# One conditioned hybrid decoder layer on 8 cores: places of its own for two row tiles, first evictions first, and a new planned order

## The reference

```python
mod = silu(c) @ w_ada + b_ada                       # six vectors: sh1, sc1, gt1, sh2, sc2, gt2
h = rmsnorm(x, norm_mix_g) * (1 + sc1) + sh1
x_rnn, y_rnn, u_pool, g_a, g_b = split(h @ w_in)    # five projections 1024 -> 1024
xr = causal_conv(x_rnn, conv_w, conv_b)             # width 4
hr = rg_lru(xr, ...)                                # gates by 4 diagonal blocks, h_t = a_t h_(t-1) + b_t
branch_a = (gelu(y_rnn) * hr) @ w_branch_a
branch_b = multiscale_pool(u_pool, ...) @ w_branch_b
x = x + gt1 * ((sigmoid(g_a) * branch_a + sigmoid(g_b) * branch_b) @ w_out)
h = rmsnorm(x, norm_mlp_g) * (1 + sc2) + sh2
x = x + gt2 * (relu(h @ w_up) ** 2 @ w_down)        # 1024 -> 4096 -> 1024
out = rmsnorm(x, final_g)
```

## Time and profile before

| what | value |
|---|---|
| runs before | 1187.74, 1188.84, 1207.44 us; median 1188.84 |
| profiled execution | 1189.46 us; span of its slowest core 1187.9 us |
| spans of the cores | 1180.7 to 1187.9 us |
| granted TensorE clock, mean of a core | 0.972 to 0.980 |
| busy | PE 1063.4 us (90%), DVE 716.0 (60%), ACT 685.5 (58%), POOL 244.6 (21%) |

### The profile page before, as it was taken

One profiled execution on the slowest core, in us unless ns is written; L12 is line 12 of the kernel. 1 busy time (PEld: TensorE's weight loads), 2 busy tenths in 40 slices (PEclk: granted clock), 3 DMA queues, 4 the chain that ended last, 5 costly groups with the idle time before them and its releaser, 6 DMA issues.

```text
span 1187.9 us, 16767 instructions; the slowest of 8 cores (1180.7 to 1187.9 us)
## 1 busy us (share of the span) xinstructions
PE 1063.4 (90%) x5262; PEld 492.6 (41%) x5262; DVE 716.0 (60%) x1060; ACT 685.5 (58%) x1054; POOL 244.6 (21%) x307
## 2 busy tenths in 40 slices
PE   0256687999999899899799999999999999999996
PEld 0123343444444344344344444444444444444442
DVE  4457877953666968977787686136403556070446
ACT  2267888575969788547888037930364211626354
POOL 2403343210413243222221013100000000022145
PEclk9888798999999999999999999999999999999998
DMA  9999775853265484416226512704030321001013
GB/s 272 229 195 203 181 193 159 232 162 119 39 161 125 71 214 88 117 27 148 45 73 199 209 72 48 131 1 72 1 71 14 58 41 31 1 18 54 18 71 124
DMA packets 46230, 127.34 MB, mean 107 GB/s; under 512 B 3888, under 2 KB 11456, under 8 KB 43840
## 3 DMA queue, kind: packets, MB, share of 16 engines
q1 hardware_dynamic: 21920, 90.82, 22.7%
q0 software_dynamic: 24224, 35.46, 20.7%
HBM read 144.93 MB, written 29.37 MB: 147 GB/s over the span
## 4 chain that ended last, share of the span: by engine, by line
PE 77%; DMA 7%; issue 5%; DVE 4%; ACT 3%; SPq 2%; POOL 1%; POOLq 0%; DVEq 0%; ACTq 0%
PE ps L579 75%; DMA w_bb<-w_b 4%; DMA ada<-w_adaT 2%; SPq L547 2%; DMA xt<-xin 1%; DVE xr L561 1%; PE ps L659 1%; ACT a L553 1%; ACT poolB L553 1%; DVE a L561 1%; POOL stat L568 1%; PE ps L912 0%; ACT L553 0%; DVE xrb L561 0%; PE ps L1094 0%
## 5 line engine op out<-in xcount | busy, mean ns | idle before, releaser
L561 DVE TENSOR_TENSOR ps<-ps,gtb 128x512 f32<-128x512 f32 x160 | 111.8, 699 | 253.1 <-PE ps L579 253.0
L579 PE MATMUL ps<-h2T,wup 128*128 128x512 bf16 x1024 | 223.5, 379 | 0.2 <-ACT h2T L553 0.2
L579 PE MATMUL ps<-wdn,ff 128*128 128x512 bf16 x1024 | 222.6, 379 | 0.0
L553 ACT ACTIVATE ps<-ps 128x512 f32<-128x512 f32 x128 | 74.0, 584 | 183.4 <-PE ps L579 183.0
L561 DVE SCALAR_TENSOR_TENSOR xr<-ps,vecs,xr 128x510 f32<-128x510 f32 (+2 forms) x192 | 135.7, 742 | 57.6 <-ACT xr L553 54.3
L579 PEld LDWEIGHTS ps<-wdn,ff 128*128 128x128 bf16 x1024 | 100.1, 98 | 120.9 <-issue 0.3
L579 PEld LDWEIGHTS ps<-h2T,wup 128*128 128x128 bf16 x1024 | 99.9, 98 | 119.8 <-issue 0.3
L561 DVE TENSOR_TENSOR x<-ps,x 128x512 f32<-128x512 f32 x160 | 110.3, 691 | 15.8 <-DVE ps L561 1.2
L568 POOL TENSOR_TENSOR thi<-thi,a 128x1024 f32<-128x1024 f32 x32 | 79.2, 2481 | 172.0 <-ACT a L553 101.1
L561 DVE TENSOR_TENSOR_SCAN a<-thr,hst,thi 128x512 f32<-128x512 f32 x64 | 85.9, 1377 | 17.3 <-POOL thi L568 17.2
L568 POOL TENSOR_SCALAR stat<-stat 128x1 f32<-128x1 f32 x65 | 18.0, 277 | 348.4 <-ACT xn L553 196.8
(11 more groups left out here) (125 smaller groups left out, 1435.5 us busy)
## 6 DMA issues: line engine op xcount, KB each, us to landing
wTb<-w_adaT SPq DMA_DIRECT2D x32, 512.0 KB, 5.2
xt<-xin SPq DMA_DIRECT2D x29, 512.0 KB, 6.9
ada<-w_adaT SPq DMA_DIRECT2D x16, 512.0 KB, 18.2
x<-xin SPq DMA_DIRECT2D x16, 512.0 KB, 10.5
yout<-x SPq DMA_DIRECT2D x16, 512.0 KB, 2.6
wdn<-w_dn POOLq DMA_DIRECT2D x6, 1024.0 KB, 13.9
wup<-w_up POOLq DMA_DIRECT2D x6, 1024.0 KB, 14.3
q_h<-hTm SPq DMA_DIRECT2D x4, 1024.0 KB, 5.6
```

The source lines that it names most:

```text
L553: N.add("act", lambda e: e.activation(out=out() if callable(out) else out, in_=in_() if callable(in_) else in_, func=func, **kw), reads=re ...
L561: return m(**args)
L579: ins = e.matmul(ps[tok.bank][:, lo:hi], lhsT=l, rhs=r, start=(first and i == 0), stop=(last and i == n - 1))
```

## The change

The rank of the first prefix tile's transposes and evictions goes from -4 to -10, so that they fall under the rule of `first`. Row tiles 2 and 3 of prefix tile 1 are loaded to two new places, `xq0` and `xq1`, which lie where `wTb1` and `wTb2` are later; tiles 0 and 1, and all rows after, keep `xt0` and `xt1`. The planner's duration of a 128x128x512 matmul is 0.2165 in place of 0.222 us and that of a transpose 0.1 in place of 0.11. `HOW` has a tilt of 14 in place of 5, three refinements in place of none, and five seeds in place of two, so the sequence of every engine is another one. The computation is the same.

```diff
-HOW = (5.0, 0, (5000001, 5000181))
+HOW = (14.0, 3, (14800055, 14800067, 14800071, 14800072, 14800142))
...
-            N.add("pe", fn, reads=reads, writes=[tok], us=0.222 * len(pairs) * (hi - lo) / 512, rank=rank, soft=soft)
+            N.add("pe", fn, reads=reads, writes=[tok], us=0.2165 * len(pairs) * (hi - lo) / 512, rank=rank, soft=soft)
...
+        xq = [at(f"xq{i}", [P, D], F32, MG + (8 + 4 * i) * K1) for i in range(2)]
+        for i in range(2):
+            reg(f"xq{i}", MG + (8 + 4 * i) * K1, 4 * K1)
+
         def norm_sub(row, s, rank):
             if row < 512:
                 t, k = xt0[s], f"xs{s}"
+            elif 512 <= row < 1024 and s > 1:
+                t, k = xq[s - 2], f"xq{s - 2}"
             else:
                 i = n_x[0] % 2
                 n_x[0] += 1
...
-                N.add("pe", tr, reads=[f"xn{s}" for s in range(nsub)] + ["ident"], writes=[tok], us=0.11 * nsub, rank=rank, soft=[keys[c]])
+                N.add("pe", tr, reads=[f"xn{s}" for s in range(nsub)] + ["ident"], writes=[tok], us=0.1 * nsub, rank=rank, soft=[keys[c]])
...
-            make_hT(T * TT, 4, lambda c: hTp[T][:, c, :], hp(T), T - 0.9 if T > 1 else -0.6 if T else -4)
+            make_hT(T * TT, 4, lambda c: hTp[T][:, c, :], hp(T), T - 0.9 if T > 1 else -0.6 if T else -10.0)
```

## The result

The changed kernel takes 1193.81 us (median of five runs, 1192.79 to 1195.48) against 1188.84 us before: a ratio of 1.0048, interval 1.0032 to 1.0064. A second series of the same file, on another chip, gave 1.0037 (1.0022 to 1.0052). So it is slower by 4.4 to 5.7 us. That is far under the 2% named in the prediction and inside its range, but on the other side of no change than the 1179.4 us forecast. Some executions of every kernel here are slow ones, with half of the chip or more at a lower granted clock; the ratios, and the times given for the experiments, are of the others.

The account below looks back on a forecast made before the run. Bound: full DMA, then ACT and DVE, with TensorE waiting, in the head; casts on DVE from 400 to 600 us. 1189.5 - 0 - 5.5 - 4 = 1180.0, or 1179.4 us for the median; range 1163 to 1197.

Parts of the forecast that it names:

- part 3: New planner order and durations, 400 to 600 us: casts on DVE set closer to the need, 4 us gained.
- Part 1: First tile's evictions go first: projections start 3.2 us earlier, at 51.1, waited away by 85 us; gain taken as 0.
- Part 2: Own places for two row tiles: x rows land earlier, TensorE's stop at 113.7 to 121.8 us goes; 5.5 us gained.
- rival (a): The forecast itself: the x-buffer stop goes and later stalls shrink, 1179.4 us (1173 to 1186); chance 0.50.
- the ring: Two xt buffers shared by nine x-row loads; with two tiles out, last main row lands near 93 instead of 119.2 us.
- rival (e): New order leaves the x loads behind the wTb wait, same time as (b); chance 0.20 together with (b).
- (b): Head: the transfer is hidden anyway, ACT and DVE take over as bound, 1188.8 us; chance 0.20, shared with rival (e).
- (c): Head: two early x rows displace weights by 5.4 us, restart at half speed adds 1.8: 1196.0 us; chance 0.15.
- (d): Search finds much more: full 9.9 us in the head and 15.2 us from 400 to 600: 1163.7 us; chance 0.13.
- Last x row before 100: Sign of being right: the last of the nine x loads lands before 100 us.
- No stop over 4 us from 100 to 130: Sign of being right, in the head: TensorE has no stop over 4 us between 100 and 130 us.
- The MLP's stretch unchanged in length: Sign of being right: the MLP, where TensorE had no idle time from 900 to 1000 us, keeps its length.

Follow-up runs that it names:

- a_wy: Changed kernel, order kept, w_y loaded in two column halves, each with its own semaphore: 1184.8 us against 1185.7 before the change, ratio 0.9997.
- a_cast: Changed kernel, order kept, four of POOL's converting copies beside the w_y load moved later: 1189.4 us against 1186.0 before the change, ratio 1.0029.
- a_wy_wb0: Changed kernel, order kept, w_y in two halves and first half of w_b behind the w_gb loads: 1181.8 us against 1185.7 before the change, ratio 0.9966.
- b_evict: Kernel before, order kept, ACT's two evictions of hTp moved ahead of the two Squares: 1188.0 us against 1186.2, ratio 1.0013.
- b_xq_sp: Kernel before, order kept, two row tiles in own places, last two x-row loads ahead of wTb loads on SP: 1187.2 us against 1186.2, ratio 1.0012.
- a_wb0: Changed kernel, order kept, first half of w_b moved behind the two w_gb loads on POOL: 1187.3 us against 1185.7 before the change, ratio 1.0016.
- a_same: Changed kernel run once more, unaltered, beside later experiments: 1191.2 us against 1186.7 before the change, ratio 1.0037.

## Why the prediction was wrong, point by point

**The step that failed is part 3**, the term of 4 us (bounds +8.2 lost, 15.2 gained). I read it from the stalls of the stretch from 400 to 600 us alone. That reading was right as far as it went: 15.2 us of idle time became 9.1, "less than 12" as the text asked, and xrb's waits 12.0 became 2.4. But I took everything outside this stretch as unchanged, and never asked what slack of the old order the new one might spend. The old order had over 38 us between the landing of w_y and its first use (45.6 in the plan); the new one has 0.3 us by the planner's price of 11.4 us for the load. The chip gave 11.3 to 19.0 us, so the load is late on five of eight cores by 2.6 to 8.0 us, and the slowest core sets the time. *a_wy* shows it as the cause of the 0.4%: with nothing else changed the loss is gone and the cores are as near each other as before. One doubt is left: in *a_cast* no core waits for w_y either, and the ratio stays at 1.0029. There w_ga is late on four cores and the head spreads the cores by 6.6 us, but no run takes these apart. The gain that the term stands for is there as well: with both late loads mended, *a_wy_wb0* is 4.0 us faster than the kernel before. That this equals my 4 us is luck in part, since no run shows which of its stages gives it. My lower bound, "one more stall of the longest kind, 8.2 us", had the right size by luck; it named a stall of DVE, and I gave it no chance of its own as a rival. No forecast case said that a load just in time is late on some cores.

**Part 1** was right in the trace and in the sum. Start forecast at 51.1, measured 51.71; worth 0, and *b_evict* alone gives 1.0013, with its start at 49.48. In the order before it is waited away for the very two landings that I named. In the changed order the third block of w_x is taken at 76.00.

**Part 2**, the term of 5.5 us, failed too: it is 0. This step is why even *a_wy*, without the loss of part 3, is level with the kernel before and not faster. *b_xq_sp* removes ACT's wait for the rows and with it the stop of the earlier trace rows, and shorter stops with other names take most of its place. The bound of 0 ("if ACT, DVE or the weights take over at once") was the truth, and the row that said so stood in my own text: ACT 87% and DVE 90% busy from 120 to 150 us. I named them against rival (a) and still took over half of the price. I was also wrong on what frees the ring. I forecast the last row to land near 93 us, but the load of the last two still leaves behind wTb, at 107.04, and the Square of the last is at 125.56 without a wait: the sequences of SP and ACT and the pace of DVE set it. That is rival (e), which I gave the time of (b). Nor would it have left near 83 us without wTb: in *b_xq_sp*, where it stands ahead of wTb, it leaves at 103.0, when ACT and DVE have used the rows before it. What the argument missed altogether is POOL's queue: a new order moves loads past each other there too, and wpl, 58.1 us from issue to landing in place of 31.5, makes a stop of 10.56 us. The planner priced that transfer at 44.6 us and the old one at 25.6, so it was short by 13.5 us on the new and by 5.9 on the old. *a_wb0* prices the stop at 0.2 to 0.3%.

**The rivals.** (b) is what parts 1 and 2 did: hidden. (c) had the nearest time, 1196.0, and the wrong mechanism: its own test, the third block of w_x taken after 88 us, reads 76.00. Half of it is there, that weights come later, but through POOL's order and not through two early x rows. (d) is ruled out for the head: idle time from 55 to 210 us did not fall (42.1 to 44.2, and 38.1 to 43.2 as the mean of the cores).

**The tests.** First projection near 51: right. Last x row before 100: wrong. No stop over 4 us from 100 to 130: wrong, 10.56. Under 12 us idle from 400 to 600: right, 9.1. The MLP's stretch unchanged in length: right, 422.5 us from its first to its last `wup` group against 421.8. No test looked at 210 to 400 us, where w_y is late. The two per cent that I took for the least that a measurement can tell were far too much: the intervals here are 0.2 to 0.5% wide.

## What to carry to other kernels

When the order of a tuned program is made anew, compare the slack of every load (landing to first use) in both orders before the stalls: a search spends slack that its model holds to be free, and it is lost on whichever core gets the bytes last. If the spans of the cores spread more than they did before, look for a transfer just in time, and give its first user less to wait for (a part with its own semaphore). And before you count a stop as a gain, look how busy the other engines are beside it: here the cause of an 8.1-us stop was taken away, one or two microseconds came back at the place, and nothing at the end.

## What the runs showed of the hardware that was not expected

- The same 2 MB load, issued within 1.5 us by the two cores of a pair, took 11.3 to 13.5 us on one and 17.7 to 19.0 on the other. In *a_same* it was 10.4 to 11.6 and 15.7 to 17.8, with the sides of all four pairs exchanged. In seven of these eight pairs the core that issued later (by 0.9 to 4.5 us) had the long time; in the eighth both issued at 382.3. (Each core's times count from its own first instruction, and how far these lie apart is not known.) With four conversions moved away on both cores the load took 7.6 to 10.0. The Trainium skill (HBM Reference, Specifications (TRN2)) says that the two cores of a pair share their memory's bandwidth. That alone gives no reason for an unequal split, and no run here had one core of a pair alone, so the cause stays open.
- A long wait of TensorE near 395 us stays in the end time of its core in full or more. Against core 7, and less what a core was late by at the issue of w_y, core 2 waits 5.3 and ends 6.0 us later, core 1 5.8 and 8.5, core 4 6.5 and 7.3, core 6 8.0 and 8.0. The restart at the lower clock, 1.5 to 1.7 us, is in that. Core 5's wait of 2.6 us leaves 0.1. Stops of 8 and 10.6 us near 120 us leave between 0 and 4. Near 120 us ACT and DVE are as short of time as TensorE; that this is the reason was only argued.
- Splitting the load made its last byte later (22 to 25 us against 11.3 to 19.0), and took 0.4% off.
